# One stage for the token-major projection, the grid convolution and the turning of the keys

## The reference, cut to what matters

```python
zx = modulate(rmsnorm(x, norm1_g), sh1x, sc1x) @ w_in       # 1024 tokens; zc the same for 256 context tokens
gq, gk, gv, gg, glr, mqk, mv, mo, mi, mf = jnp.split(zf, idx, axis=-1)
...
img = t.reshape(bsz, rows, grid_w, ch)                      # t = mqk, ch = 1024, depthwise 3x3
y = lax.conv_general_dilated(img, w, (1, 1), 'SAME', feature_group_count=ch, ...)
qk = jax.nn.silu(y + b)
mq, mk = jnp.split(qk, 2, axis=-1)                          # 512 channels of queries, 512 of keys
```

## Time and profile before

| | |
|---|---|
| median of 3 runs | 4398.53 us (4390.68 to 4402.25) |
| profiled execution | 4391.63 us, its span 4390.0 us |
| busy TensorE, VectorE, ScalarE, GpSimd | 78%, 48%, 27%, 4% of the span |
| granted TensorE clock, mean | 0.887 of full speed |

### The profile page before, as it was taken

The page is one execution under the profiler, slowest core; times in us unless marked ns, Lnnn a source line. Parts: engine busy times, 40 slices in busy tenths (PEclk is TensorE's granted clock), DMA queues, the critical chain, the costliest instruction groups (busy, mean ns, idle before and its releaser), DMA issues. The chain is left out here.

```text
span 4390.0 us, 52510 instructions
## 1 busy us (share of the span) xinstructions
PE 3438.7 (78%) x18825; PEld 2720.3 (62%) x18826; DVE 2098.2 (48%) x2999; ACT 1188.0 (27%) x1808; POOL 184.2 (4%) x262
## 2 busy tenths in 40 slices
PE   7599882077585898988847987974947998998977
PEld 1388772066364777766625876962835887787855
DVE  0411014834523756577743113836643775576543
ACT  0401002123422645566622002333122110011021
POOL 1000000013101000000010000000000000000000
PEclk9799995578796999999968998996978999999988
DMA  7232210349454967699922322111020332232211
GB/s 249 71 93 85 84 58 12 102 155 244 162 188 181 326 235 277 238 333 333 336 92 67 96 86 72 40 39 51 4 72 25 95 94 83 86 91 86 86 52 44
DMA packets 394400, 562.01 MB, mean 128 GB/s; under 512 B 43373, under 2 KB 277540, under 8 KB 394148
## 3 DMA queue, kind: packets, MB, share of 16 engines
q1 hardware_dynamic: 350392, 431.46, 30.6%
q10 hardware_dynamic: 26784, 69.74, 4.4%
q0 software_dynamic: 17104, 59.17, 3.6%
HBM read 451.51 MB, written 108.79 MB: 128 GB/s over the span
## 5 line engine op out<-in xcount | busy, mean ns | idle before, releaser
L1760 DVE TENSOR_TENSOR exp_w_lo<-exp_w_raw,exp_w_hi 128x1024 fp32r<-128x1024 f32 x384 | 450.4, 1221 | 145.9 <-ACT exp_w_hi L1734 143.4
L1734 ACT ACTIVATE exp_w_hi<-exp_w_raw 128x1024 fp32r<-128x1024 f32 x384 | 382.1, 1051 | 176.5 <-DMA exp_w_raw<-in_expert_w_in 155.9
L325 PE MATMUL in_ps_psum<-hN_hi,in_wh 128*128 128x512 f32 x704 | 276.1, 392 | 40.0 <-DVE in_wl L319 40.0
L325 PE MATMUL up_ps_psum<-hN_hi,up_wh 128*128 128x512 f32 x704 | 281.6, 400 | 31.2 <-DVE up_wl L319 31.2
L326 PE MATMUL up_ps_psum<-hN_lo,up_wh 128*128 128x512 f32 x704 | 281.1, 399 | 0.0
L327 PE MATMUL up_ps_psum<-hN_hi,up_wl 128*128 128x512 f32 x704 | 280.9, 399 | 0.0
L326 PE MATMUL in_ps_psum<-hN_lo,in_wh 128*128 128x512 f32 x704 | 275.7, 392 | 0.0
L327 PE MATMUL in_ps_psum<-hN_hi,in_wl 128*128 128x512 f32 x704 | 275.2, 391 | 0.0
L325 PE MATMUL exp_up_psum<-exp_w_hi,exp_x_hi 128*128 128x512 f32 x592 | 235.9, 399 | 11.1 <-DVE exp_w_lo L1760 10.4
L317 DVE CAST in_wh<-in_w 128x1024 fp32r<-128x1024 f32 x44 | 30.5, 694 | 425.6 <-PE in_ps_psum L327 414.2
L326 PE MATMUL exp_up_psum<-exp_w_lo,exp_x_hi 128*128 128x512 f32 x592 | 231.4, 391 | 0.0
(11 more groups left out here) (604 smaller groups left out, 7534.9 us busy)
## 6 DMA issues: line engine op xcount, KB each, us to landing
exp_w_raw<-in_expert_w_in SPq DMA_DIRECT2D x256, 512.0 KB, 5.4
exp_w_raw<-in_expert_w_out SPq DMA_DIRECT2D x128, 512.0 KB, 6.1
up_w<-in_ffn_up SPq DMA_DIRECT2D x88, 512.0 KB
moe_rows<-zero_rows ACTq DMA_DIRECT2D x50, 512.0 KB, 2.7
ada_w<-in_ada_w SPq DMA_DIRECT2D x12, 2048.0 KB, 8.0
in_w<-in_w_in SPq DMA_DIRECT2D x44, 512.0 KB, 4.2
down_w<-in_ffn_down SPq DMA_DIRECT2D x44, 512.0 KB
exp_rows<-moe_rows POOLq DMA_DIRECT2D x39, 512.0 KB, 7.7
```

Of the source, the lines that this page charges most:

```text
L325: pe.matmul(out, r(w[0]), r(x[0]), start=start, stop=False)
L1734: act.activation(wh[:, c, :].bitcast(F32R), raw[r][:], ACT.Copy).then_inc(s_wh, 1)
L1760: dve.tensor_tensor(wl[:, c, :].bitcast(F32R), raw[r][:], wh[:, c, :], ALU.subtract).then_inc(s_wl[r], 1)
```

## The change

`stage_gemm_t` for these groups, `stage_conv` and `stage_turn_rows` become one stage, `stage_values`, at the place of the first. `mixer_one` no longer calls the other two. The weights come through a ring of 4 slices with a semaphore each; ScalarE makes the high part, VectorE the low part. Key channels are convolved first (`tile(j) = (j + 4) % 8`); images, accumulators and the one buffer `rows` are double- or single-buffered as shown. `stage_misc` and `stage_gates` follow, then `stage_gla` directly.

```diff
-def stage_conv(K):           (all of it, with the hardware loops)
-def stage_turn_rows(K, name, src, ncols, dst, src0=0):      (all of it)
+def stage_values(K, name, groups, toks):
+    R, W, NB, NR, NC, NTAP = 16, 64, 4, 4, D // P, 12
+        wh, wl = sb("wh", [P, KT, BANK]), sb("wl", [P, KT, BANK])
+        rows = sb("key_rows", [P, NCH, P])
+        pm = [K.ps(f"{name}_ps{i}", [P, BANK], st) for i in range(NB)]
+        pt = K.ps(f"{name}_turn", [P, 12, P], st)
...
+            def _(sp):
+                def weights(g, ks): ...      # slice m = g * KT + k: if m >= NR: wait s_wl >= m - NR + 1; load
+                def image(j):
+                    if j < 2:
+                        sp.wait_ge(s_z, 4)
+                    else:
+                        sp.wait_ge(s_tap, 9 * (j - 1))
+                        sp.wait_ge(s_ctx, 3 * (j - 1))
...
+                weights(0, range(KT))
+                image(0)
+                image(1)
+                weights(1, range(NR))
+                image(2)
+                image(3)
+                image(4)
+                weights(1, range(NR, KT))
+                image(5)
+                weights(2, range(NR))
+                image(6)
+                image(7)
+                weights(2, range(NR, KT))
...
+            def _(pe):
+                def turn(j):
+                    pe.wait_ge(s_act, j + 1)
+                    if j:
+                        pe.wait_ge(s_tc, j)
+                    for n in range(NCH):
+                        mm = pe.transpose(pt[:, n, :], acc[j % 2][:, n * P:(n + 1) * P], K.c("ident"))
...
+                        if m in (4, 6, 8, 11):
+                            turn((4, 6, 8, 11).index(m))
...
+            def _(act):
+                def weights(g): ...          # if g: wait s_mm >= nt * g; per slice: wait its load; Copy to wh
+                def convolved(j):
+                    act.wait_ge(s_tap, 9 * (j + 1))
+                    act.wait_ge(s_ctx, 3 * (j + 1))
+                    act.activation(acc[u][:], acc[u][:], ACT.Silu, ...).then_inc(s_act, 1)
+                    act.wait_ge(s_act, j + 1)
+                    (two stores to mqkF, on s_cs[u])
+                def turned(j):
+                    act.wait_ge(s_t, j + 1)
+                    if j:
+                        act.wait_ge(s_ts, 32 * j)
+                    act.activation(rows[:], pt[:, 0:NCH, :], ACT.Copy).then_inc(s_tc, 1)
+                    act.wait_ge(s_tc, j + 1)
+                    (two stores to mkT, on s_ts)
+                for m in range(nt * NG_):
+                    if m % nt == 0:
+                        weights(m // nt)
+                    evict(m)
+                    if m in (3, 5, 7, 10, 13, 15, 17, 20):
+                        convolved((3, 5, 7, 10, 13, 15, 17, 20).index(m))
+                    if m in (5, 7, 9, 12):
+                        turned((5, 7, 9, 12).index(m))
...
+            def _(dve):
+                def convolve(j):
+                    dve.wait_ge(s_in[u], 32 * (j // 2 + 1))
+                    if j >= 2:
+                        dve.wait_ge(s_cs[u], 32 * (j // 2))
+                        dve.wait_ge(s_t, min(j - 1, 4))
+                    for tap in range(9):
+                        (the grid tap; from the second on it waits for the tap before it)
+                        if 3 <= tap < 6:
+                            (a context tap)
+                weights(0)
+                for j in range(4):
+                    convolve(j)
+                weights(1)
+                for j in range(4, 8):
+                    convolve(j)
+                weights(2)
...
-        stage_gemm_t(K, "vT", [(part(GV, 512), vT, 0), (part(MV, 512), vT, 512), (part(GK, 256), gkT, 0)], toks, bufs=1)
+        stage_values(K, "vT", [(part(GV, 512), vT, 0), (part(MV, 512), vT, 512), (part(GK, 256), gkT, 0)], toks)
...
-    stage_conv(K)
-    stage_turn_rows(K, "mkT", K.scratch["mqkF"], 512, K.dram("mkT", [TSCAN, 512]), src0=512)
```

More of the change, by code:

```diff
@@ L787, in backwards @@
     return bass.AP(a.tensor, a.offset + n - 1, [a.ap[0], [-1, n]])
-def stage_conv(K):
+def stage_values(K, name, groups, toks):
     nc = K.nc
-    raw, out = K.scratch["mqk_raw"], K.dram("mqkF", [1024, TSCAN])
-    R, W = 16, 64
-    U = range(4)
+    raw, out, mkT = K.scratch["mqk_raw"], K.dram("mqkF", [1024, TSCAN]), K.dram("mkT", [TSCAN, 512])
+    R, W, NB, NR, NC, NTAP = 16, 64, 4, 4, D // P, 12
+    nt, NG_ = len(toks), len(groups)
+    tile = lambda j: (j + 4) % NC
     with K.stage() as st:
[L797 to L803, removed]
+        U = range(2)
+        sb = lambda n, shape: K.sb(f"{name}_{n}", shape, stack=st)
+        wt, ob = [sb(f"w{i}", [P, BANK]) for i in range(NR)], [sb(f"out{i}", [P, BANK]) for i in range(NB)]
+        wh, wl = sb("wh", [P, KT, BANK]), sb("wl", [P, KT, BANK])
+        img, row, acc = [sb(f"img{u}", [P, R + 2, W + 2]) for u in U], [sb(f"ctxrow{u}", [P, NCTX + 2]) for u in U], [sb(f"conv{u}", [P, TALL]) for u in U]
+        rows = sb("key_rows", [P, NCH, P])
+        pm = [K.ps(f"{name}_ps{i}", [P, BANK], st) for i in range(NB)]
+        pt = K.ps(f"{name}_turn", [P, 12, P], st)
+        s_w, s_o = [K.sem(f"{name}_w{i}") for i in range(NR)], [K.sem(f"{name}_o{i}") for i in range(NB)]
+        s_in, s_cs = ([K.sem(f"{name}_{n}{u}") for u in U] for n in ("conv_in", "conv_stored"))
+        s_z, s_wh, s_wl, s_mm, s_ev, s_tap, s_ctx, s_act, s_t, s_tc, s_ts = (K.sem(f"{name}_{n}") for n in (
+            "zero", "wh", "wl", "mm", "ev", "taps", "ctx_taps", "silu", "turned", "rows", "rows_stored"))
+        stored = [0] * NB
         with nc.Block() as block:
@@ L812, in _, with weights @@
             def _(sp):
[L813 to L820, removed]
+                def weights(g, ks):
+                    w = groups[g][0]
+                    n = w.shape[1]
+                    for k in ks:
+                        m = g * KT + k
+                        if m >= NR:
+                            sp.wait_ge(s_wl, m - NR + 1)
+                        sp.dma_start(wt[m % NR][:, 0:n], w[k * P:(k + 1) * P, :]).then_inc(s_w[m % NR], 16)
@@ new lines, in image @@
+                def image(j):
+                    u, c = j % 2, slice(tile(j) * P, tile(j) * P + P)
+                    if j < 2:
[3 more added lines that the diff above has]
+                        sp.wait_ge(s_ctx, 3 * (j - 1))
+                    sp.dma_start(img[u][:, 1:R + 1, 1:W + 1], raw[c, NCTX:NCTX + T].rearrange("p (r w) -> p r w", w=W)).then_inc(s_in[u], 16)
+                    sp.dma_start(row[u][:, 1:NCTX + 1], raw[c, 0:NCTX]).then_inc(s_in[u], 16)
@@ new lines, in _ @@
+                weights(0, range(KT))
[11 more added lines that the diff above has]
+                weights(2, range(NR, KT))
+            @block.tensor
+            def _(pe):
[5 more added lines that the diff above has]
+                        mm = pe.transpose(pt[:, n, :], acc[j % 2][:, n * P:(n + 1) * P], K.c("ident"))
+                    mm.then_inc(s_t, 1)
+                for g, (w, dst, c0) in enumerate(groups):
+                    n = w.shape[1]
+                    for i, (src, t0, _) in enumerate(toks):
+                        m = g * nt + i
+                        if m >= NB:
+                            pe.wait_ge(s_ev, m - NB + 1)
+                        t = slice(t0, t0 + P)
+                        for k in range(KT):
+                            if i == 0:
+                                pe.wait_ge(s_wl, g * KT + k + 1)
+                            mm = matmul3(pe, pm[m % NB][:, 0:n], (src[0][:, k, t], src[1][:, k, t]), (wh[:, k, 0:n], wl[:, k, 0:n]),
+                                         start=k == 0, stop=k == KT - 1)
+                        mm.then_inc(s_mm, 1)
+                        if m in (4, 6, 8, 11):
+                            turn((4, 6, 8, 11).index(m))
@@ new lines, in _, with weights, evict @@
+            @block.scalar
+            def _(act):
+                def weights(g):
+                    n = groups[g][0].shape[1]
+                    if g:
+                        act.wait_ge(s_mm, nt * g)
+                    for k in range(KT):
+                        m = g * KT + k
+                        act.wait_ge(s_w[m % NR], 16 * (m // NR + 1))
+                        act.activation(wh[:, k, 0:n].bitcast(F32R), wt[m % NR][:, 0:n], ACT.Copy).then_inc(s_wh, 1)
+                def evict(m):
+                    b, (w, dst, c0) = m % NB, groups[m // nt]
+                    n = w.shape[1]
+                    act.wait_ge(s_mm, m + 1)
+                    if stored[b]:
+                        act.wait_ge(s_o[b], stored[b])
+                    act.activation(ob[b][:, 0:n], pm[b][:, 0:n], ACT.Copy).then_inc(s_ev, 1)
+                    act.wait_ge(s_ev, m + 1)
+                    for r in toks[m % nt][2]:
+                        act.dma_start(dst[r:r + P, c0:c0 + n], ob[b][:, 0:n]).then_inc(s_o[b], 16)
+                        stored[b] += 16
+                def convolved(j):
```

(46 more changed lines are left out.)

## The result

The changed kernel takes 4253.19 us (median of 4 runs, 4248.72 to 4260.4) against 4395.2 us for the kernel before on the same chip (4390.68 to 4402.25): ratio 0.9675, interval 0.9659 to 0.9692. The profiled execution took 4255.09 us, span 4253.6 us, so 136.4 us less than the profiled one of before. A second comparison, 5 runs against 9, gave 0.9679 (0.9656 to 0.9701).

A forecast was written before the change was run, and what follows sets the result against it. Bound by TensorE in the projection, then VectorE in the convolution, barriers making times add. Removed -142.2, added -4.5 + 6.4 + 2.6 + 1.8 = +6.3, total -135.9: 4255.7 us profiled, 4262.6 from the median, forecast 4260, range 4244 to 4286.

The forecast's parts named there:

- Removed: Convolution and key-turning stages with their barriers, between gates and scan, disappear: -142.2 us.
- Start: Fused stage's beginning: slice 0 suffices to start, so token tile 0 completes at about 496.5: -4.5 us, bounds 0 and -6.
- Turns: Four turns of ten key transposes on TensorE between token tiles, 1.6 us each with hand-over: +6.4 us, bounds 5.5 to 10.
- First tile of group 1: Token tile 10: key copy on ScalarE and late ring loads make it 12.3 us: +2.6 us, bounds 0 and +6.
- First tile of group 2: Token tile 20: same ring, no key copy ahead, 7.9 us against 6.1 before: +1.8 us, bounds 0 and +5.
- Convolution: VectorE's taps in the fused stage cost nothing, covered by TensorE; room 9 us in first half, 1 in second.
- VectorE as the bound: Rival: slower convolution tiles on VectorE exceed the fused stage's room; 4265 to 4275 us, say 4269; chance 0.13.
- the fall of the clock at turns: Rival: transposes let TensorE's clock drop, about 3.5 us a turn, 14 us in all: 4274 us; chance 0.06.
- ScalarE's order: Rival: key stores or held issues lengthen `turned` by 4 us and stall TensorE: +4 to +15, 4270 us; chance 0.08.
- No overlap: Rival: the convolutions' 96 us are added to the fused stage, 40 us saved, 4358 us; chance 0.02.
- slower than before: Rival: taps starve beside TensorE, ScalarE and DMAs; at 3.3 us a tap total about 4440 us; chance 0.01.

The follow-up runs named there:

- the bare ring: Changed kernel with convolution and turns moved back to stages of their own, only the ring of 4 weight slices kept: 4397.23 us, stage 159.3 us.
- the last experiment: Changed kernel with six ring places instead of four, 4250.49 us; then also the third key copy behind eviction 10 instead of 9, 4243.23 us.
- both edits: Changed kernel with six ring places and the third key copy behind eviction 10 instead of 9: 4243.23 us, ratio to the kernel before 0.9657.

## Why the prediction was right

The forecast was 4260 with the range 4244 to 4286 and 135.9 us saved. The main mechanism, the convolution hidden under TensorE and the keys turned between tiles, is what the traces show, and most of its terms held singly:

- *Removed, 142.2 us.* The gates stage runs straight into the scan. The two stages between took 0.6 and 0.4 us more than before, 29.46 and 96.31 us.
- *Start, -4.5.* Tile 0 was complete 12.7 us into the stage instead of 17.8: -5.1.
- *Turns, +6.4.* The eviction behind the first turn comes after 6.58 us instead of 5.44, the one behind the last after 6.55; between them ScalarE's own queue shifts the evictions, and a turn shows over two tiles. The four cost 1.14, 1.11, 1.14 and 1.11, 4.5 us together. Full clock and no hand-over: the estimate of 0.2 for that was not needed, and 1.4 for ten was itself taken too high, since 1.10 for eight included the fill.
- *First tile of group 1, +2.6.* 13.5 us against the forecast 12.3 and 9.6 before: +3.9. The sequence was right: key copy at +1.1, first slice rounded from +3.5, then waits for the late slices' loads of 2.09, 0.77 and 0.54 us. The size of the loads was off: the last slice was rounded from 561.13 and not from 560, since it landed 4 us behind the end of SP's issues at 557.06, beside the image that SP issued next, at a DMA share of 0.94. TensorE's clock fell here too (0.72 between 556 and 560), but in this kernel that is nearly hidden behind the loads: TensorE ended 1.05 us behind the last slice, and 1.45 in the second execution.
- *First tile of group 2, +1.8.* +2.2 in one execution, +1.1 in the other; behind it 0.6 at tile 21 and 0.1 at the end in the first, by where the clock's fall lies.
- *Convolution, 0.* One channel tile took 11.9 us for the 12.0 worked out, a dependent tap 1.31 us. VectorE was done 60.8 and 125.8 us into the stage, forecast 61.8 and 128.8. The room in the second half, counted as in the prediction up to TensorE's tile 19, was 2.8 us instead of 1 (4.35 up to the first rounded slice), as tile 10 took longer on TensorE while VectorE began its next tile 77.4 us into the stage (forecast 78.5), and as the wait for the store was 0.56 instead of 2. One more tap fitted into it, three more found its end. What the comparison with the bare ring leaves open is at most 1.2 us at tile 10, by way of the clock and not of a tap.

Measured terms: -5.1 + 4.5 + 3.9 + 2.2 + 0.7 = +6.2, against +6.3 forecast. That the sum is so close is luck in part, since the first three terms miss by 0.6, 1.9 and 1.3 us in different directions.

Of the rivals, VectorE as the bound (0.13) and the fall of the clock at turns (0.06) did not occur; clock falls there are, but at TensorE's waits, and the prediction has no term for them. They account for the 0.6 us behind tile 21 and for part of the scatter at tile 20. ScalarE's order (0.08) was no stall in the midst of groups, but at m = 9 it costs what the last experiment gives back: part of that rival was true and already in the sum. No overlap, and slower than before, did not occur: 96 us of taps beside a working TensorE kept their durations.

What stays open: the timed medians show 142.0 and 140.4 us saved, the traces 136.4, and the traces alone from stage start to scan 135.0 and 136.2. Both intervals of the ratio include 0.9691, which is 136 us. The stages behind the scan's start are the same code in every kernel, and took 3479.4 us in the profiled execution of before, 3476.3 and 3476.8 in the two of the changed kernel, and between 3466.7 and 3490.6 in the ten profiled executions of this study. With such a scatter 5 us more or less on the whole can't be ascribed.

## What to carry to other kernels

A stage that keeps one engine busy and a stage that keeps another busy, with a barrier between, are worth up to the shorter of the two if their dependencies allow it; work out the room per stretch between two synchronising points (here the weights of the next group), not over the stage, and test it by adding idle work until it shows. What costs in the fused stage is then the shared go-between: look at what stands in its queue ahead of the instruction that restarts the busy engine, and move it behind. And a wait of the busy engine can cost more than its length, when it comes back at half clock with work ready. Here six ring places alone gave 3.2 to 4.9 us, and taking the long copy out from ahead of the restart gave 3.6 more.

## What the runs showed of the hardware

- Ten fp32 transposes at full clock cost 1.11 to 1.14 us between matmuls, and 40 of them in a row (4.5 us) left the granted clock at 1.00. In the kernel before it rose from 0.55 (112 to 116 us) to 1.00 (116 to 120) under nothing but transposes.
- The granted clock was 0.50 from 549 to 552 us behind a TensorE wait of 5.1 us (six ring places), and stayed at 1.00 behind one of 2.6 us at the same place of the program (both edits); in the kernel with the turns split off it fell in a wait of 2.10 us. A matmul of 256 columns started every 0.21 instead of 0.12 us at half clock.
- Taps of 1.28 us on VectorE (median 1.284, before 1.280) did not lengthen beside TensorE, ScalarE and a DMA share of 0.54 (0.38 in the old convolution stage).
- Loads of the context row, 128 KB issued right behind an image, kept SP's queue for 1.3 to 3.4 us each, where a weight slice took 0.43 us in the median and 1.1 at most. The first tap waited 1.5 us for one, in VectorE's room; in the changed kernel TensorE never waited for a tap.
